# Modulation weights loaded as tiles of 128 rows by 1024 columns in a two-layer transformer kernel

## The reference, cut to what matters

```
cond = silu(c)                                  # 1024 values
for l in range(2):
    mod = cond @ ada_w[l] + ada_b[l]            # ada_w[l]: 1024 x 6144
    sh1, sc1, g1, sh2, sc2, g2 = split(mod, 6)
    h = rms_norm(x, norm_mix[l]) * (1 + sc1) + sh1
    x = x + g1 * (mixer(h) @ w_out[l])
    h = rms_norm(x, norm_ffn[l]) * (1 + sc2) + sh2
    x = x + g2 * swiglu(h)
```

## Time and profile before

| | us |
|---|---|
| median of 3 runs | 2844.66 (2844.15 to 2855.97) |
| profiled execution, span of its instructions | 2849.3 |
| its time outside the span | not given by the profile |
| PE busy (matmul) | 2693.0 |
| POOL, DVE, ACT busy | 1236.4, 1150.2, 1076.1 |

### The profile page before, as it was taken

One profiled execution on the slowest core, in us unless ns is written; L12 is line 12 of the kernel. 1 busy time (PEld: TensorE's weight loads), 2 busy tenths in 40 slices (PEclk: granted clock), 3 DMA queues, 4 the chain that ended last, 5 costly groups with the idle time before them and its releaser, 6 DMA issues.

```text
span 2849.3 us, 34441 instructions
## 1 busy us (share of the span) xinstructions
PE 2693.0 (95%) x13145; PEld 2149.3 (75%) x13145; DVE 1150.2 (40%) x1788; ACT 1076.1 (38%) x1728; POOL 1236.4 (43%) x652
## 2 busy tenths in 40 slices
PE   6997899999999899999999999999999997999998
PEld 5775567888876578888788888888888763788886
DVE  3168743222127632221236656233321488433312
ACT  3333543332237633332345555333322333433321
POOL 2322533444424334444345655444444485444442
PEclk8998989999999899999999999999999998999998
DMA  8654502223321013323221211223323110232321
GB/s 274 212 168 142 177 30 85 93 88 100 102 79 45 31 61 108 97 88 107 78 74 60 74 50 56 89 92 100 103 87 102 63 59 30 69 109 88 99 96 56
DMA packets 275967, 265.16 MB, mean 93 GB/s; under 512 B 20268, under 2 KB 274829, under 8 KB 275853
## 3 DMA queue, kind: packets, MB, share of 16 engines
q1 hardware_dynamic: 275853, 263.59, 29.2%
HBM read 261.47 MB, written 2.10 MB: 93 GB/s over the span
## 4 chain that ended last, share of the span: by engine, by line
PE 81%; DVE 11%; ACT 3%; issue 2%; SPq 1%; POOL 0%; DMA 0%; DVEq 0%; ACTq 0%
PE bank L1253 20%; PE bank L1255 20%; PE bank L1254 20%; DVE bank L2402 3%; PE bank L985 1%; PE bank L1277 1%; PE bank L987 1%; PE bank L986 1%; PE bank L1279 1%; PE bank L1278 1%; PE bank L1007 1%; PE bank L976 1%; PE bank L977 1%; PE bank L978 1%; PE bank L1357 1%
## 5 line engine op out<-in xcount | busy, mean ns | idle before, releaser
L849 POOL TENSOR_TENSOR w_lo<-w_raw,w_hi 128x1024 fp32r<-128x1024 f32 (+1 forms) x364 | 864.0, 2384 | 1276.0 <-ACT w_hi L1903 739.3
L1253 PE MATMUL bank<-h_hi,w_hi 128*128 128x512 f32 x1632 | 644.1, 395 | 19.1 <-DVE h_lo L2558 12.4
L1254 PE MATMUL bank<-h_lo,w_hi 128*128 128x512 f32 x1632 | 639.8, 392 | 0.0
L1255 PE MATMUL bank<-h_hi,w_lo 128*128 128x512 f32 x1632 | 639.4, 392 | 0.0
L1903 ACT ACTIVATE w_hi<-w_raw 128x1024 fp32r<-128x1024 f32 (+1 forms) x232 | 233.7, 1021 | 481.7 <-PE bank L1255 436.9
L1253 PEld LDWEIGHTS bank<-h_hi,w_hi 128*128 128x128 f32 x1632 | 309.6, 190 | 88.7 <-issue 19.7
L1254 PEld LDWEIGHTS bank<-h_lo,w_hi 128*128 128x128 f32 x1632 | 309.5, 190 | 65.8 <-issue 1.7
L1255 PEld LDWEIGHTS bank<-h_hi,w_lo 128*128 128x128 f32 x1632 | 309.3, 190 | 65.4
L1253 PE MATMUL bank<-a_hi,w_hi 128*128 128x512 f32 x704 | 273.9, 389 | 0.0
L1254 PE MATMUL bank<-a_lo,w_hi 128*128 128x512 f32 x704 | 273.9, 389 | 0.0
L1255 PE MATMUL bank<-a_hi,w_lo 128*128 128x512 f32 x704 | 273.9, 389 | 0.0
(11 more groups left out here) (385 smaller groups left out, 4392.5 us busy)
## 6 DMA issues: line engine op xcount, KB each, us to landing
ada_w<-in_ada_w_dram SPq DMA_DIRECT2D x96, 512.0 KB, 6.1
w_raw<-in_ffn_gate_dram SPq DMA_DIRECT2D x22, 1024.0 KB, 5.3
w_raw<-in_ffn_up_dram SPq DMA_DIRECT2D x22, 1024.0 KB, 5.3
w_raw<-in_ffn_w_gate_dram SPq DMA_DIRECT2D x22, 1024.0 KB, 5.3
w_raw<-in_ffn_w_up_dram SPq DMA_DIRECT2D x22, 1024.0 KB, 5.2
w_raw<-in_ffn_down_dram SPq DMA_DIRECT2D x16, 1024.0 KB, 5.1
w_raw<-in_ssm_w_in_dram SPq DMA_DIRECT2D x16, 1024.0 KB, 5.3
w_raw<-in_ffn_w_down_dram SPq DMA_DIRECT2D x16, 1024.0 KB, 5.1
```

The costliest lines, as they stand in the source:

```text
L849: pool.tensor_tensor(w_lo[parity][:, 0:nk, half], w_raw[parity][:, 0:nk, half], w_hi[parity][:, 0:nk, half].bitcast(F32), ALU.subtract).th ...
L1253: pe.matmul(dst[m][:], hi, src_hi(k0 + k), start=first and k == 0, stop=False)
L1254: pe.matmul(dst[m][:], hi, src_lo(k0 + k), start=False, stop=False)
L1255: ins = pe.matmul(dst[m][:], lo, src_hi(k0 + k), start=False, stop=last and k == nk - 1)
```

## The change

A tile is now 128 rows by 1024 columns, `[128, 1024]`, each partition one contiguous 4 KB of DRAM. There are still 96 tiles of 512 KB, in the same places and in the same order of places; eight tiles (one per chunk of 128 rows) make a block of 1024 columns, and there are 12 blocks, 2 of them in the head and 6 in the projection.

The four matmuls of a tile share one column of `cond`; strip j takes columns 256j to 256j+255 of the tile and accumulates over the eight tiles in columns 0 to 255 of bank 7. So the four strips are four pieces of the row, and nothing has to be summed across them. A copy takes 128 x 256. Two transposes of 128 x 128 put the row into columns 256 to 511 of bank 7, and the take reads eight columns from there with a stride (`ada_turned`), in the order that `mod` wants (`ada_columns_of`). `ada_pick` and its five memsets go.

In the head, `norm_sums` and `spread` are tied to block 1 of 2 now: the sums stand before the rows of tiles 9 to 16, as before, and the spreading after all of them, ahead of the columns of block 1. In the projection a block is copied after every odd slot and turned in every even one; in the attention it is copied every sixth step and turned every sixth.

```diff
-ADA_BLOCKS, ADA_FIRST, ADA_PROJ = 24, 4, 16
+ADA_TILES, ADA_W = 8, 1024
+ADA_BLOCKS, ADA_FIRST, ADA_PROJ = 12, 2, 8
-        ada_w = {kb: in_big(f"ada_w{kb}", [P, 4, SLOT_W], kb) for kb in ADA_EARLY}
-        ada_row = in_big("ada_row", [P, 2 * SLOT_W], 54)
+        ada_w = {kb: in_big(f"ada_w{kb}", [P, ADA_W], kb) for kb in ADA_EARLY}
+        ada_row = in_big("ada_row", [P, ADA_W // 4], 54)
+        def ada_columns_of(ap):
+            return ap.rearrange("p (j c) -> p c j", c=2)
+        def ada_turned():
+            return bank[7][:, ADA_W // 4:ADA_W // 2].rearrange("p (c j r) -> p c j r", c=2, j=4)[:, :, :, 0]
+            def load_ada(v):
+                b, k = divmod(v, ADA_TILES)
+                l, c0 = divmod(b * ADA_W, 6 * D)
...
+                sp.dma_start(ada_w[buf][:], t["ada_w"][l, P * k:P * k + P, c0:c0 + ADA_W]).then_inc(ada_full[buf], 16)
-            for g in range(5):
-                load_ada(g)
+            for v in range(10):
+                load_ada(v)
...
+            def ada_rows(v):
...
+                if k == 0 and b >= 1:
+                    pe.wait_ge(ada_added, b)
+                pe.wait_ge(ada_full[buf], 16 * (len(users) + 1))
                 for j in range(4):
-                    ins = pe.matmul(bank[7][32 * j:32 * j + 32, at:at + SLOT_W],
-                                    cond[:, 4 * half + j:4 * half + j + 1].to_broadcast([P, 32]), ada_w[buf][:, j, :],
-                                    start=half == 0, stop=half == 1)
+                    ins = pe.matmul(bank[7][32 * j:32 * j + 32, 0:w], cond[:, k:k + 1].to_broadcast([P, 32]),
+                                    ada_w[buf][:, w * j:w * j + w], start=k == 0, stop=k == ADA_TILES - 1)
             def ada_columns(b):
                 pe.wait_ge(ada_copied, b + 1)
-                for j in range(4):
-                    ins = pe.matmul(bank[7][:, j:j + 1], ada_row[:, P * j:P * j + P], ada_pick[:], start=True, stop=True)
+                for c in range(2):
+                    at = ADA_W // 4 + P * c
+                    ins = pe.transpose(bank[7][:, at:at + P], ada_row[:, P * c:P * c + P], ident[:])
             for b in range(ADA_FIRST):
-                if b == 2:
+                if b == 1:
                     norm_sums(0)
-                ada_block(b)
-                if b == 2:
+                for k in range(ADA_TILES):
+                    ada_rows(ADA_TILES * b + k)
+                if b == 1:
                     spread(0)
                 ada_columns(b)
-                    if s % 3 == 0 and s // 3 <= ADA_BLOCKS - ADA_PROJ:
-                        ada_columns(ADA_PROJ + s // 3 - 1)
+                    if s % 6 == 0 and s // 6 <= ADA_BLOCKS - ADA_PROJ:
+                        ada_columns(ADA_PROJ + s // 6 - 1)
+            def within_even(s):
+                if s % 2 == 0:
+                    ada_columns(ADA_FIRST + s // 2 - 1)
             def index_relu(s):
-                ada_copy(ADA_FIRST + s)
+                if s % 2 == 1:
+                    ada_copy(ADA_FIRST + s // 2)
```

More of the change, by code:

```diff
@@ L112, in ada_places @@
     order = list(ADA_EARLY)
[L113 to L116, removed]
+    while len(order) < ADA_TILES * ADA_PROJ:
+        order.append(ADA_MIDDLE[(len(order) - ADA_TILES * ADA_FIRST) % len(ADA_MIDDLE)])
+    while len(order) < ADA_TILES * ADA_BLOCKS:
+        order.append(ADA_LATE[(len(order) - ADA_TILES * ADA_PROJ) % len(ADA_LATE)])
     return order
 ADA_PLACES = ada_places()
-N_CONSTS = 20
+N_CONSTS = 15
 AHEAD = 2
@@ L613, in load_slot @@
                                  src.rearrange("(k p) m -> p k m", p=P)).then_inc(w_full[n % 2], 16)
[L615 to L624, removed]
+            def load_ada(v):
+                b, k = divmod(v, ADA_TILES)
+                l, c0 = divmod(b * ADA_W, 6 * D)
+                buf, users = ada_tile(v)
+                if users:
+                    sp.wait_ge(ada_used, users[-1] + 1)
+                if v >= ADA_TILES * ADA_PROJ and buf in (24, 28):
+                    sp.wait_ge(idx_summed, len(idx_units))
+                sp.dma_start(ada_w[buf][:], t["ada_w"][l, P * k:P * k + P, c0:c0 + ADA_W]).then_inc(ada_full[buf], 16)
             def load_swiglu(f):
@@ L665, in _ @@
                     later_loads()
[L666 to L669, removed]
+                for v in range(4):
+                    load_ada(ADA_TILES * ADA_FIRST + 4 * n + v)
+            for v in range(ADA_TILES * ADA_PROJ, ADA_TILES * ADA_BLOCKS):
+                load_ada(v)
             for m in range(2, 4):
@@ L1364, in ada_columns @@
                 pe.wait_ge(ada_copied, b + 1)
-                for j in range(4):
-                    ins = pe.matmul(bank[7][:, j:j + 1], ada_row[:, P * j:P * j + P], ada_pick[:], start=True, stop=True)
+                for c in range(2):
+                    at = ADA_W // 4 + P * c
+                    ins = pe.transpose(bank[7][:, at:at + P], ada_row[:, P * c:P * c + P], ident[:])
                 ins.then_inc(ada_col, 1)
-            def ada_block(b):
-                for g in (2 * b, 2 * b + 1):
-                    for half in range(2):
-                        ada_rows(g, half)
             pe.wait_ge(consts, 2)
@@ L1621, in attention @@
                         tile_back((s - 27) // 2)
-                    if s % 3 < 2 and s // 3 < ADA_BLOCKS - ADA_PROJ:
-                        for half in range(2):
-                            ada_rows(2 * (ADA_PROJ + s // 3) + s % 3, half)
+                    if s % 3 < 2 and s // 6 < ADA_BLOCKS - ADA_PROJ:
+                        for v in range(2):
+                            ada_rows(ADA_TILES * ADA_PROJ + 4 * (s // 3) + 2 * (s % 3) + v)
             def index_scores(v):
@@ L1635, in after_even @@
             def after_even(s):
-                ada_block(ADA_FIRST + s)
+                for v in range(4):
+                    ada_rows(ADA_TILES * ADA_FIRST + 4 * s + v)
                 if s == 2:
@@ L2877, in _ @@
             dve.wait_ge(ada_added, ADA_BLOCKS)
-            late = slice(4 * ADA_FIRST, 4 * ADA_BLOCKS)
-            link(dve.tensor_tensor(mod[:, late], mod[:, late], col_range("ada_b", 4 * ADA_FIRST, 4 * (ADA_BLOCKS - ADA_FIRST)),
-                                   ALU.add))
+            late = slice(ADA_TILES * ADA_FIRST, ADA_TILES * ADA_BLOCKS)
+            link(dve.tensor_tensor(mod[:, late], mod[:, late],
+                                   col_range("ada_b", ADA_TILES * ADA_FIRST, ADA_TILES * (ADA_BLOCKS - ADA_FIRST)), ALU.add))
             make_gain(1, 32, "norm_ffn", 0)
```

54 lines of the change are left out of this document (24 added, 30 removed).

## The result

The kernel after takes 2813.15 us (median of 4 runs, 2810.98 to 2816.19) against 2848.28 of the kernel before beside it (2844.15 to 2855.97): ratio 0.9876, 95% interval 0.9854 to 0.9898. The prediction started from 2844.66, the median of three runs of before; with the fourth it is 2848.28, so 3.6 us of the gap are the starting point. The profiled executions differ by 34.8 us (span 2849.3 and 2814.5), and these are compared here, cut at the same instruction of each: the first product of slot 0, DVE's root that starts its unbroken work, the first bias add of the attention, the first product of the output projection, the output's first store.

What follows compares the result with a forecast made beforehand. Bounds: head by bytes, projection by PE, end of top-k by DVE, attention by a ring of engines with PE busiest. Head 3.5 + projection 8.3 + attention 7 = 18.8 us off 2844.66 gave 2825.9 us; 8-in-10 range 2817 to 2837.

Steps and rivals of the forecast that it cites:

- The pieces: Head: 4 KB pieces in place of 1 KB load the sixteen tiles 3.8 us sooner.
- rival 2: Head: larger pieces don't speed the tiles, by a memory-side limit; 2829.7 us, or 2831.2 with `spread` at half clock; chance 0.11.
- The work behind the landing: Head, after the last tile lands: 2.6 us becomes 2.9, between 2.3 at full and 4.4 at half clock; 0.3 lost.
- The lambda wait: Projection, slot 2: ACT's exponent starts sooner, so the lambda matmul's 2.01 us wait shrinks by 0.85.
- a sign against me: End of the top-k, 190.6 to 264.9 us: if it shrinks, DVE did not bound it; no gain was predicted.
- I take half: Attention: 14.5 us if PE alone sets the pace, 0 if DVE does; half taken, 7 us.
- The term of the columns: Attention: four column groups that go save 5.0 us; the four that stay take 0.4 each for 1.05.
- The term of the waits: Attention: four waits for ACT's copy that go save 6.1 us; those that stay have a copy shorter by 0.2.
- Rival 3: Attention: PE falls to half clock and the kernel gets slower, +21 us, 2866; chance 0.04.
- My sign of being wrong: Behind the attention: the distance from its end to the program's end moves by over 2 us.
- Rivals 1: Attention: the ring holds its pace, only 1.5 us of the first wait are won; 2831.4 us; chance 0.20.
- Rival 4: Attention and head: all 14.5 us won and the low stretches between tiles closed; 27 us, 2818; chance 0.07.

Runs made afterwards that it cites:

- apart1k: Kernel after, each partition's 4 KB of a tile read as four 1 KB pieces 6 KB apart in DRAM: 2817.64 us, ratio 0.9896.
- full: Kernel after with the attention's late-sum work of before (four products, copy of 512, half-block waits at eight steps): 2829.71 us, ratio 0.9942.
- the second pair: Both kernels profiled once more, unedited: before 2849.92 us; after 2813.18 us, ratio 0.9887.
- full_two: `full` with two one-column products in place of four at each of the eight attention steps: 2821.30 us, ratio 0.9920.
- before_half: Kernel before without the attention's late-sum groups at s = 3, 9, 15 and 21: 2834.45 us, ratio 0.9953.
- full_narrow: `full` with the attention's ACT copy of 256 columns in place of 512: 2826.39 us, ratio 0.9941.

## Why the prediction was wrong

The spans differ by 34.8 us in place of 18.8. The 16.0 us between are 9.0 in the attention, 7.8 behind it and 1.3 in the top-k, less 1.0 in the head and 1.1 in the projection.

- **The head** (3.5 predicted, 2.5 measured). The pieces were right: 402 GB/s, last tile 3.5 us sooner, and `apart1k` takes it back, so rival 2 falls. The Trainium skill ("DMA: Bandwidth & Descriptors", Specifications) gives 512 B as the least transfer for line rate, by which 1 KB would do as well as 4 KB; the runs disagree, 351 against 402 GB/s. The work behind the landing was mis-sized: 2.9 is not the middle of 2.3 and 4.4, which is 3.35, and it took 3.7 us, on PE wholly at half clock, so that 1.0 us was lost there and not 0.3. In `full`, which has the same head, this work met the full clock: the spreading took 1.16 us in place of 2.08 and slot 0 started at 44.82. Which of the two clocks this work meets differs from execution to execution.
- **The projection** (8.3 and 7.2). PE's busy time from slot 0 to the root fell by 5.6 us (138.4 to 132.8; 5.0 in the second pair) for 5.8 worked out, and its idle time by 1.7 (in both pairs) for 2.5. The wait of slot 1 is gone. The lambda wait fell by 0.2 (2.01 to 1.80) in place of 0.85: ACT's exponent came 0.94 sooner against PE's last work, but DVE's next tiny operation took 0.88 us in place of 0.15.
- **The end of the top-k** (0 and 1.3). I named a shrinking as a sign against me, and it shrank: from 72.2 us in all three executions with the projection of before to 70.9 in all thirteen of the others. DVE does bound the stretch (busy for 67.8 of 72.9 us). What I missed is that its operations need not keep their length: two neighbouring ones took 3.60 us before and 2.33 after (rows in the last section), and all others kept theirs to 0.1.
- **The attention** (7 and 12.7 to 16): the step that failed is "I take half". The 14.5 us that I had halved, all waits and columns as if PE alone set the pace, is near what was won (14.8 and 13.4 in the first four parts of the two pairs), but partly by luck. The term of the columns was right: 7.6 us in the sum (5.0 and 2.6), 7.2 and 7.5 measured. The term of the waits (6.1 and 0.8) was not: PE's idle time fell by 1.7 and 1.0 only. The four waits that stay took 4.9 us before and 5.8 and 5.1 after, not 0.8 less, and the others came back as waits for the other engines. (The 13.3 us of the earlier trace rows are those of PE's weight loads; PE itself waited 11.0.) In place of the waits stands a term that the sum put at nothing: 7.0 and 4.2 us of PE's busy time from a higher clock. The argument for half, DVE's share, held in the widest units: the third part won -0.4 and 1.0 us in two pairs of executions, though a wait and a column group left it. But they are 25 of 123 us. In the fourth part, where DVE was busy for 18.05 of 31.07, it had no force. There PE's busy time fell from 26.60 to 20.89: 1.05 and 0.61 for products less, which leaves 24.94; that at 0.84 of the clock is 20.9 at 1.00. So 4 of 8.2 us are clock and 1.7 products, the rest waits (in the second pair about 3 of 7.1 are clock).
- **The clock.** Rival 3 asked whether PE falls to half clock with fewer pauses, and I kept 0.8 to 0.9 in the forecast. It stayed there (0.88 and 0.90), but within that band it rose from 0.82 and 0.86. The fourth part of `full` and `full_two` shows the sign: with groups of a wait and four one-column products the half clock came on behind them, and with two products it stayed away. No term of the sum stood for that.
- **Behind the attention** (0 and 7.8). My sign of being wrong, a move of over 2 us, was met, but it was a bad sign: that stretch takes 2443 to 2457 us over all profiled executions, and moves by 3.3 us between two of the same kernel. Here before, `before_half`, whose head is that of before, and `full_narrow`:

```profile
388.43:2842.30 2453.87, 2368.88 (x10966) 1920.28 (x10964) 939.23 (x1324) 912.34 (x1368) 1109.12 (x548) 0.97 0.25 79
```

```profile
379.67:2826.00 2446.33, 2361.14 (x10966) 1913.06 (x10964) 939.01 (x1324) 910.69 (x1368) 1108.66 (x548) 0.98 0.25 79
```

```profile
370.50:2824.60 2454.10, 2370.11 (x10966) 1921.09 (x10964) 939.15 (x1324) 911.34 (x1368) 1109.37 (x548) 0.97 0.25 79
```

 The same instructions take 8 us more or less with 0.01 of mean clock. That belongs to an execution. Whether after draws the better level more often than before (in both pairs it did, by 7.8 and 13.6 us), and so whether some of the 35 us is this, stays open: against medians of before of 2844.5 after is 31.3 us faster, of 2848.3 35.1, while head, projection, top-k and attention explain 23 to 27.

Rivals 1 and 3 fall with the attention. Rival 4 was nearest in time, with all 14.5 of it, but not by its reasons: it had no clock in it, and the head, whose low stretches it closed, won 2.5 us and not more than 3.5.

## What to carry to other kernels

When an overhead stands between stages with different limits, cut the stretch at the overhead itself and ask for each part which engine fills it; a limit seen in the widest units says nothing for the rest. A wait taken out of a ring of engines need not be time won: ask who is waited for next. An interruption of PE (a wait and then a few matmuls that stream little) costs its own time and can cost the clock of the work behind it: here 4 to 7 us beside 7 of the matmuls themselves. A total can't tell whether a 2 us edit worked when the unchanged part of the program varies by more, up to 14 us between profiled executions here: compare the stretch.

## What the runs showed of the hardware

- Tiles of 512 KB on one queue load at 351 to 354 GB/s in pieces of 1 KB (four executions, from 12 to 20 us) and at 386 to 411 in pieces of 4 KB (twelve; 402 in after). Pieces written apart but lying side by side in memory become one (239,102 packets, not 275,965).
- The narrow loads that follow are not sped up by the room the tiles leave: 223 GB/s before, 216 after.
- DVE operations of one shape vary several times over with what POOL does. The last two operations of a top-k of 384 columns, and POOL's beside them, before and then after:

```profile
231.44 1.02 DVE L2750 TENSOR_SCALAR score<-score 128x384 f32<-128x384 f32 x1
232.50 2.58 DVE L2751 TENSOR_TENSOR dist_sel<-score,dist 128x384 f32<-128x384 f32 x1
229.89 4.77 POOL L849 TENSOR_TENSOR w_lo<-w_raw,w_hi 128x1024 fp32r<-128x1024 f32 x2 [16.30 <-ACT w_hi L1903]
```

```profile
221.69 1.77 DVE L2757 TENSOR_SCALAR score<-score 128x384 f32<-128x384 f32 x1
223.50 0.56 DVE L2758 TENSOR_TENSOR dist_sel<-score,dist 128x384 f32<-128x384 f32 x1
218.57 4.68 POOL L852 TENSOR_TENSOR w_lo<-w_raw,w_hi 128x1024 fp32r<-128x1024 f32 x2 [15.62 <-ACT w_hi L1905]
```

The long one of each pair ends 0.2 to 0.4 us behind the end of POOL's work (235.08 and 234.66 before, 223.46 and 223.25 after). The tiny operation of the lambda, the difference of two exponents, took 0.15 us before, when POOL had just finished, and 0.88 after, when it ended together with POOL's at 85.14. So these rows look like DVE waiting for POOL; no run took POOL's work away to test it.
